# The first projection by input tile: another order of the first loads, of the first matmuls and of VectorE's first work

## What is computed

```python
hn = rms_norm(h, mixer_norm_g[layer])
proj = h @ w_in                                   # 1024 x 2560
q, k, v, g, u = jnp.split(proj, [512, 1024, 1536, 2048], axis=-1)
q = rope(q, positions)                            # t1*cos - t2*sin, t1*sin + t2*cos
k = rope(k, positions) * (Dh ** -0.5)
scores = jnp.einsum('bhncd,bhnmd->bhncm', qc, kc) * decay_mask[:, None]
o_intra = jnp.einsum('bhncm,bhnme->bhnce', scores, vc)
pool_out = multiscale_pool(u, pool_w, pool_scale) # windows of 2, 4, 8, 16 tokens
```

## Times and profile before

| | us |
|---|---|
| median of 3 runs (1122.77 to 1123.47) | 1122.93 |
| profiled execution, device time | 1124.2 |
| its span in the trace | 1122.4 |
| TensorE busy | 1115.6 (99%) |
| VectorE busy | 834.2 (74%) |
| ScalarE busy | 610.5 (54%) |
| GpSimd busy | 44.4 (4%) |
| all DMA queues | 203.53 MB, mean 181 GB/s |

### The profile page before, as it was taken

The page is one execution under the profiler, slowest core; times in us unless marked ns, Lnnn a source line. Parts: engine busy times, 40 slices in busy tenths (PEclk is TensorE's granted clock), DMA queues, the critical chain, the costliest instruction groups (busy, mean ns, idle before and its releaser), DMA issues.

```text
span 1122.4 us, 18843 instructions
## 1 busy us (share of the span) xinstructions
PE 1115.6 (99%) x7338; PEld 995.4 (89%) x7338; DVE 834.2 (74%) x1287; ACT 610.5 (54%) x951; POOL 44.4 (4%) x67
## 2 busy tenths in 40 slices
PE   9999999999999999999999999999999999999998
PEld 9999888888876988888899998888888789888887
DVE  6977877766775878777658867877765887877753
ACT  5645566554541756655543455666544677655631
POOL 4030000000000000000000000000001210000000
PEclk9999999999999999999999999999999999999999
DMA  8545555555483445555544645555654325555552
GB/s 306 189 158 183 175 194 189 195 194 184 154 282 112 151 168 208 188 188 200 210 153 153 223 151 187 188 188 190 220 191 150 136 91 185 186 192 189 181 201 69
DMA packets 35368, 203.53 MB, mean 181 GB/s; under 512 B 4176, under 2 KB 10576, under 8 KB 11984
## 3 DMA queue, kind: packets, MB, share of 16 engines
q1 hardware_dynamic: 35136, 202.32, 51.4%
q10 hardware_dynamic: 144, 0.01, 0.0%
HBM read 200.09 MB, written 2.23 MB: 180 GB/s over the span
## 4 chain that ended last, share of the span: by engine, by line
PE 94%; DVE 3%; DMA 1%; ACT 1%; issue 0%; SPq 0%; DVEq 0%; ACTq 0%
PE banks L421 46%; PE banks L434 24%; PE banks L397 5%; PE banks L403 5%; PE banks L400 5%; PE banks L474 5%; PE banks L457 1%; PE banks L463 1%; PE banks L460 1%; DMA raw_t<-w 1%; DVE lo_t L328 1%; PE banks L1610 0%; DVE lo_t L315 0%; DVE scr L1369 0%; PE banks L1596 0%
## 5 line engine op out<-in xcount | busy, mean ns | idle before, releaser
L328 DVE TENSOR_TENSOR lo_t<-raw_t,hi_t 128x1024 fp32r<-128x1024 f32 x364 | 439.9, 1220 | 11.4 <-ACT hi_t L322 10.3
L322 ACT ACTIVATE hi_t<-raw_t 128x1024 fp32r<-128x1024 f32 x364 | 376.1, 1050 | 106.2 <-PE banks L434 39.1
L421 PE MATMUL banks<-x,hi_t 128*128 128x512 f32 x1536 | 363.4, 391 | 0.0
L421 PEld LDWEIGHTS banks<-x,hi_t 128*128 128x128 f32 x1536 | 284.1, 188 | 57.2 <-issue 0.8
L434 PEld LDWEIGHTS banks<-x,lo_t 128*128 128x128 f32 x1536 | 193.5, 191 | 5.4
L434 PE MATMUL banks<-x,lo_t 128*128 128x256 f32 x1536 | 195.8, 283 | 0.0
L421 PE MATMUL banks<-f,hi_t 128*128 128x512 f32 x704 | 164.1, 390 | 0.0
L421 PEld LDWEIGHTS banks<-f,hi_t 128*128 128x128 f32 x704 | 130.6, 188 | 26.1
L560 DVE TENSOR_TENSOR scr<-banks,scr 128x512 f32<-128x512 f32 x88 | 60.9, 692 | 82.0 <-ACT scr L628 81.3
L434 PEld LDWEIGHTS banks<-f,lo_t 128*128 128x128 f32 x704 | 87.6, 192 | 1.9
L434 PE MATMUL banks<-f,lo_t 128*128 128x256 f32 x704 | 88.2, 283 | 0.0
(11 more groups left out here) (197 smaller groups left out, 1117.6 us busy)
## 6 DMA issues: line engine op xcount, KB each, us to landing
raw_t<-w SPq DMA_DIRECT2D x182, 1024.0 KB, 4.9
scr<-shifts SPq DMA_DIRECT2D x32, 142.0 KB, 4.1
raw_t<-w SPq DMA_DIRECT2D x3, 512.0 KB, 10.2
shifts<-scr SPq DMA_DIRECT2D x8, 144.0 KB, 3.5
h<-xT SPq DMA_DIRECT2D x4, 256.0 KB, 7.7
out<-h SPq DMA_DIRECT2D x8, 128.0 KB, 4.4
cst<-consts SPq DMA_DIRECT2D x1, 816.0 KB, 12.4
raw_t<-w SPq DMA_DIRECT2D x2, 256.0 KB, 5.1
```

The source lines that it names most:

```text
L322: e.activation(hi_t[:, p % RING, :], raw_of(p), ACT.Copy).then_inc(s_hi, 1)
L328: e.tensor_tensor(lo_t[:, p % RING, :], raw_of(p), hi_t[:, p % RING, :].bitcast(F32), ALU.subtract).then_inc(s_lo, 1)
L421: m = e.matmul(halves(banks[:, to[j], :]), hi_t[:, slot, r * P:(r + 1) * P], parts[:, ks[j], :, :], start=ks[j] == 0 and not low_first, st ...
```

## The change

The whole query and key projection is taken by input tile, with eight weight tiles (one piece) for each, into banks 0 to 3. The weights' layout on the host follows (`wide(tiles(...), 8)`). SyncE's list is reordered: x's second, third and fourth transfers go later, the fourth behind chunk 2; the first half piece is issued by ScalarE. The column sums stand before input tile 6, root's spread behind V's first two strips. On VectorE x's low parts 5 to 7 and the low parts of pieces 5 to 8 go between the angle's operations, and the mean as well. ScalarE waits for the columns and the gains' product behind high part 8, where it waits for the angles. The warm-up has 17 matmuls.

```diff
-WARM_START = 21
+WARM_START = 17
...
             e.dma_start(h[:, 0:2, :], xT[:, 0:2, :]).then_inc(s_x[0], 16)
-            e.dma_start(raw_t[:, 0, 0:512], w[0, :, 0:512]).then_inc(s_first[0], 16)
             e.dma_start(raw_t[:, 0, 512:PIECE], w[0, :, 512:PIECE]).then_inc(s_first[1], 16)
-            for n in range(1, EARLY):
...
+            for what in ("w1", "x1", "w2", "w3", "x2"):
...
             load_chunk(e, 2)
+            e.dma_start(h[:, 6:8, :], xT[:, 6:8, :]).then_inc(s_x[3], 16)
...
         def act_start(e):
+            e.dma_start(raw_t[:, 0, 0:512], w[0, :, 0:512]).then_inc(s_first[0], 16)
             e.dma_start(col[:, 0:FIRST_COLS], cols[:, 0:FIRST_COLS]).then_inc(s_col0, 16)
...
                 act_xh(e, 0, k)
-                early_hi(e, k)
-            for p in range(EARLY, RING):
-                split_hi(e, p)
-            e.wait_ge(s_col, 16)
-            e.wait_ge(s_gg, 1)
+                if k < EARLY:
+                    early_hi(e, 2 * k)
+                    early_hi(e, 2 * k + 1)
+                elif k < RING:
+                    split_hi(e, k)
...
         def dve_start(e):
             e.memset(one[:, :], 1.0).then_inc(s_one, 1)
-            for k in range(KD):
+            for k in range(EARLY):
                 dve_xl(e, 0, k)
-                early_lo(e, k)
+                early_lo(e, 2 * k)
+                early_lo(e, 2 * k + 1)
+            dve_xl(e, 0, 4)
             split_lo(e, EARLY)
+            dve_xl(e, 0, 5)
+            lo_to(e, 19)
...
+            dve_xl(e, 0, 6)
+            lo_to(e, 27)
             e.wait_ge(s_col, 16)
...
-            lo_to(e, 19)
+            dve_xl(e, 0, 7)
+            lo_to(e, 35)
+            dve_mean(e, 0)
             for c in (P1, P2, P3, P4):
...
+            lo_to(e, 48)
...
         def pe_first_tiles(e, k):
...
+            for half in range(2):
+                js = range(4 * half, 4 * half + 4)
+                dsts = [banks[:, j // 2, (j % 2) * T:(j % 2 + 1) * T] for j in js]
...
         def pe_retention(e):
             for k in range(KD):
+                if k == 6:
+                    pe_col_sums(e, 0)
                 pe_first_tiles(e, k)
-            for u in range(2, 4):
...
             for k in range(KD):
                 strip(e, G_V + 4 * k, (banks[:, 4, :], banks[:, 5, :]), k, k == 0, k == KD - 1)
+                if k == 0:
+                    pe_spread(e, 0)
...
         def act_retention(e):
             hi_to(e, 35)
+            e.wait_ge(s_col, 16)
+            e.wait_ge(s_gg, 1)
             e.wait_ge(s_angle, 2)
             e.activation(sin, w1, ACT.Sin, scale=colv("sgn", 0))
             e.activation(cos, w0, ACT.Sin).then_inc(s_sines, 1)
-            for u, c in zip(range(4), (51, 59, 67, 75)):
+            for u, c in zip(range(4), (64, 67, 71, 75)):
                 hi_to(e, c)
                 ps = banks[:, u, :]
-                e.wait_ge(s_tiles, upto(16 * max(u, 1) + 15))
+                e.wait_ge(s_tiles, upto(63))
...
         def dve_retention(e):
-            lo_to(e, 48)
-            dve_mean(e, 0)
...
-    parts = [wide(tiles(w_in[:, 0:1024]), 4), flat(strips(w_in[:, 1024:1536])), flat(tiles(w_in[:, 2048:2560])),
+    parts = [wide(tiles(w_in[:, 0:1024]), 8), flat(strips(w_in[:, 1024:1536])), flat(tiles(w_in[:, 2048:2560])),
```

More of the change, by code:

```diff
@@ L727, in act_start @@
             e.activation(st[:, 5, 0:1], one[:, 0:1], ACT.Copy)
+            e.wait_ge(s_col0, 16)
             for k in range(KD):
-                if k == 0:
-                    e.wait_ge(s_col0, 16)
                 if k % 2 == 0:
@@ L814, in pe_first_tiles @@
         def pe_first_tiles(e, k):
-            half, at = k % 2, k // 2 + 1
-            dsts = [banks[:, v, t * T:(t + 1) * T] for v in range(2) for t in range(2)]
-            cols_of = [slice((4 * half + j) * P, (4 * half + j + 1) * P) for j in range(4)]
-            e.wait_ge(s_hi if half else s_hi_half, at)
-            e.wait_ge(s_xh, x_done(0, k))
-            for j in range(4):
-                e.matmul(dsts[j], hi_t[:, k // 2, cols_of[j]], x2[:, k, 0, :], start=k == 0 and j % 2 == 0, stop=False,
-                         skip_group_check=True)
@@ L824, in pe_first_tiles @@
-            e.wait_ge(s_xl, x_done(0, k))
-            for j in range(4):
-                e.matmul(dsts[j], hi_t[:, k // 2, cols_of[j]], x2[:, k, 1, :], start=False, stop=False,
-                         skip_group_check=True)
-            e.wait_ge(s_lo if half else s_lo_half, at)
-            for j in range(4):
-                m = e.matmul(dsts[j], lo_t[:, k // 2, cols_of[j]], x2[:, k, 0, :], start=False, stop=k == KD - 1,
-                             skip_group_check=True)
-            if half:
-                m.then_inc(s_tiles, 1)
+            for half in range(2):
+                js = range(4 * half, 4 * half + 4)
+                dsts = [banks[:, j // 2, (j % 2) * T:(j % 2 + 1) * T] for j in js]
+                cols_of = [slice(j * P, (j + 1) * P) for j in js]
+                early = k < EARLY and half == 0
+                e.wait_ge(s_hi_half if early else s_hi, k + 1)
+                e.wait_ge(s_xh, x_done(0, k))
+                for j, dst, c in zip(js, dsts, cols_of):
+                    e.matmul(dst, hi_t[:, k % RING, c], x2[:, k, 0, :], start=k == 0 and j % 2 == 0, stop=False, skip_group_check=True)
+                e.wait_ge(s_xl, x_done(0, k))
+                for dst, c in zip(dsts, cols_of):
+                    e.matmul(dst, hi_t[:, k % RING, c], x2[:, k, 1, :], start=False, stop=False, skip_group_check=True)
+                e.wait_ge(s_lo_half if early else s_lo, k + 1)
+                for dst, c in zip(dsts, cols_of):
+                    m = e.matmul(dst, lo_t[:, k % RING, c], x2[:, k, 0, :], start=False, stop=k == KD - 1, skip_group_check=True)
@@ L835, in pe_retention @@
+            m.then_inc(s_tiles, 1)
         def pe_retention(e):
             for k in range(KD):
+                if k == 6:
+                    pe_col_sums(e, 0)
                 pe_first_tiles(e, k)
-            for u in range(2, 4):
-                for t in range(2):
-                    for k in range(KD):
-                        c = 16 * u + 8 * t + k
-                        if c == 48:
-                            pe_col_sums(e, 0)
-                        if c == 60:
-                            pe_spread(e, 0)
-                        tile(e, G_QK + c, banks[:, u, t * T:(t + 1) * T], k, x2, k == 0, k == KD - 1)
```

10 lines of the change are left out of this document (6 added, 4 removed).

## The result

The changed kernel took 1127.45 us (median of 5 runs, 1126.72 to 1127.51) beside 1122.93 us for the one before (5 runs, 1122.3 to 1124.24): a ratio of 1.0035 with a 95% interval of 1.0025 to 1.0046, slower by 4.5 us, where 1126.7 was forecast. Timed again later (e8) it took 1125.88 (11 runs) beside 1123.1 (33 runs), a ratio of 1.0023 (1.0014 to 1.0031), slower by 2.8. The profiled execution took 1127.08 with a span of 1125.3, 2.9 over the span before.

A forecast was written before the change was run, and what follows sets the result against it. VectorE's serial chain, not TensorE at 99% busy, was taken as the thin place. Waits of 2.55 at U's first low part, then 0.2, reaching 3.8 in total at PV, took 1122.9 to 1126.7 us; range 1124.3 to 1128.2.

The forecast's parts named there:

- rival A: Chunk 3 lands 1.6 to 2.0 us earlier and VectorE's chain follows one for one: 1124.7 us; chance 0.17.
- its own signs of being wrong: Chunk 3 landing before 23, the table load running before the angles, or VectorE beginning low part 12 before 44.
- Part 1: Shorter warm-up and earlier first values: TensorE starts at 7.7, 0.9 us earlier; columns 0.3 later, hidden; bounds 0 and 1.0.
- the 0.55 of stops at piece 6: TensorE at input tile 6: high part ready at 26.2 against 25.9, and the low part costing 0.25 us.
- Part 2: Order of the input stream: two TensorE stops of 0.3 to 0.7 us stay, at pieces 2 and 4; joint bounds 0 and 1.6.
- Part 3: Landing of the next weights, chunk 3: 25.1 us, bounds 23.1 to 26.1; V begins at 32.2, 2.45 earlier.
- its two terms of 1.5 and 0.4: Lower bound of chunk 3's landing: 1.5 us by which its issue can move up, 0.4 from the first half piece's issue.
- Part 4: VectorE's chain to the sines: angles at 33.4 (now 27.4), table load behind them, low part 9 late by 4.4 us.
- the 0.55 of slack: Before PV in the old kernel: third head's masked scores ready at 72.30, PV matmuls beginning at 72.89.
- B: Faster: input stops were the bound and the angles' chain is not, 1120.5 us; chance 0.06.
- C: TensorE's long stop at U also costs speed, +2.9 us, of which 1.05 lies in VectorE's lag: 1128.5; chance 0.11.
- D: Angles late, but ScalarE's table load out of the chain: -1.3 us, 1125.4, still slower; chance 0.08.

The follow-up runs named there:

- e8: Changed kernel timed again, unaltered, beside the kernel before; 1125.88 us, 1.0023 to the kernel before.
- e2: Changed kernel with a small early sine, so ScalarE loads the sine table ahead of its waits; 1124.24 us, 1.0011 to the kernel before.
- e5: e3 with VectorE's last eight angle operations moved ahead, four before x's low part 6 and four behind low part 6; 1122.21 us, 0.9991 to the kernel before.
- e1: Changed kernel with the first half piece back on SyncE's list, behind x's first transfer; 1125.32 us, 1.0019 to the kernel before.
- e9: Changed kernel with ScalarE issuing the small column load ahead of the first half piece; 1125.58 us, 1.0020 to the kernel before.
- e7: Kernel before with only the warm-up shortened, 17 matmuls for 21; 1122.77 us, 0.9998 to the kernel before.
- e4: Kernel before with only the first half piece issued by ScalarE, ahead of the columns; 1125.73 us, 1.0023 to the kernel before.
- e6: e5 with low parts 12 to 14 earlier among the ropes and 19, 20 in VectorE's waits for GpSimd; 1122.26 us, 0.9989 to the kernel before.
- e3: Changed kernel with the edits of e1 and e2 together; 1123.67 us, 1.0006 to the kernel before.

## Why the prediction was right, and where its terms were not

**Direction and cause: right. Size: near, and in part by luck.** The stretch to PV was forecast 3.8 us longer and is 2.9 longer. The main cause is the one named, VectorE's serial chain with the angles behind the low parts, and ScalarE's table load behind the angles. e2 and e5 show it: each link taken out comes back at PV, 1.35 and 1.47. But 1.05 more comes from the late start, which the prediction had hidden. Without it (e1's start, at full clock behind U) PV would stand 1.9 over before, 75.40 - 0.65 against 72.89, which by the prediction's own scale is 1124.8, rival A's time and not the forecast's. One of its own signs of being wrong also came true: chunk 3 landed before 23. And the waits that it looked for ahead of high and low part 9 are not in TensorE's rows; with V early they are (e1: 0.61 and 0.60).

**Part 1, the start: wrong.** The columns were to be 0.3 us late, with a bound of 1.0, and hidden. They were 3.4 late, and TensorE began at 9.33, not 7.7, though the warm-up did end at 7.64. The step that failed counted the cost of the second queue as 0.3 us, an issue's time. What it left out is what a small transfer pays behind a large one on the same queue: e9 takes that away with one swap. V began at 33.85 instead of 32.2, late by these 1.6 us; the length from the first matmul to V came out as reckoned (24.5), though the 0.55 of stops at piece 6 in it are not there.

**Part 2: within its bounds.** Two stops of 0.3 to 0.7 were forecast. One has a row, 0.46, ahead of a low part at input tile 4; the one at piece 2 is not there, nor is it in e1, where TensorE starts at 7.15.

**Part 3, chunk 3: wrong, without effect.** It landed at 22.50, not 25.1 (bounds 23.1 to 26.1; 25.1 less its two terms of 1.5 and 0.4 is 23.2). The step read the share of 0.99 as "the same bytes take the same time". A share says that the DMA engines are busy, not how much they move: from 9 to 12 us the share was 0.94 before and 1.04 after, and the rate 269 and 424 GB/s. Nor did the full share bear out the bound set beside it, that the landing moves by 0.4 us at most: it moved by 2.8 (25.27 to 22.50).

```profile
9.00:12.00 3.00, 3.00 (x28) 3.00 (x27) 0.83 (x3) 1.39 (x3) 2.02 (x3) 1.00 0.94 269
```
```profile
9.00:12.00 3.00, 2.67 (x22) 2.67 (x23) 3.00 (x4) 3.00 (x7) 2.17 (x4) 1.00 1.04 424
```

The landing also varies without any change to the stream, 25.27 in the profile of before and 24.17 in e7's. SyncE issued the chunk at 14.38, not near 11.5, since the two pieces of chunk 0 were split later.

**Part 4, the chain: its length right, its start right by two errors that cancel, which is luck.** It was to start with chunk 3, low part 6 at 26.2. Chunk 3 was there 3.7 us sooner, but VectorE was not: it had begun at 8.79 and not stood still, its operations beside GpSimd taking up to twice their time (x's low part 0.95, alone 0.48). Low part 6 began at 25.79. From there the working holds: to the last angle operation 6.9 us (7.1), to the high part behind the load 2.0 (2.02), to low part 9 1.15 (1.1). +3.8 instead of +4.4 there is the 0.4 of low part 6's start and the 0.2 of the chain. The spread and piece 9 cost 0.1 us and not 1.9, because V began 1.6 later while the chain was 0.6 earlier; as the prediction has it, all of this is gone at U anyway. The stop at U was 2.12, ahead of PV +3.5 arrived of +3.8, less the 0.55 of slack: 2.9. The 0.3 went into a wait that the prediction had counted as none: before, VectorE stands 0.26 for TensorE at 57.28, and after the change it does not.

**The medians.** At equal mean clock 1.000, on one chip, the changed kernel takes 1125.47 (5 runs) and the one before 1122.93 (20 runs): 2.5 us. With both slow stretches the changed kernel takes 1127.03 (3 runs). In the first measurement all five runs of it had a slow stretch and four had both, hence 4.5; in the second three of eleven had both, hence 2.8. With the 1.2 and 0.65 of the two stretches, 2.5 becomes 4.35 of the 4.5. So the forecast of 3.8 lies between the two levels, and hits the first median closely only because the clock added what the chain did not.

**The rivals.** A (chunk 3 early, and the chain one for one with it): the landing came, the gain did not, since VectorE was held by its own start. With the start repaired (e1) low part 6 does follow the chunk, which lands at 23.57, 1.5 before the forecast's time, and the cost over before is 1.7 at equal mean clock (1124.43 in 4 runs against 1122.70). B (faster): no; even e5, with all links out, gains 0.9 us, not 2.4. C (the stop costs speed too): wrong for the profiled execution, right as a mechanism in at least 21 of 49 runs, four of the first five among them, at a lower price: the stretch from U's first low part to PV takes 28.67 us in e1 and 27.52 in the changed kernel without its last wait, 1.15 more where 2.9 was put, and 0.65 of it is left at PV where 1.85 was put, since the rest goes into that wait. Its remark that the granted clock is 1.00 throughout holds for the rows that it cites, to 27 us; the same trace has 0.50 at 364. D (table load not in the chain): no; e2 is that case, made, and costs 1.3 less, as D was priced.

## What to carry to other kernels

Before work is moved into an engine's stream, ask which other engine waits for what stands behind it, and count that wait with all that it holds up: here the angles moved by 5 us on VectorE, and a table load and three high parts on ScalarE went with them. Use the first function of a new table ahead of the wait for its data. A small transfer on which everything starts goes first on its queue; a stop of TensorE may, in some executions, cost its clock as well as its length. And repair an unrelated delay before judging an order: here the late start hid how early the chunk was there.

## What was not expected of the hardware

- 256 KB ahead of 9 KB on ScalarE's queue delayed the 9 KB by 3.4 us and x's first transfer on SyncE's queue by 2.6 (4.75 to 7.34; in e4 by 1.3, to 6.09); the reverse order delayed both by under 0.4.
- In the changed kernel's profile the DMA engines moved 80 GB/s at a share of 0.64 (4 to 5 us), 129 at 1.02 (3 to 4 us) and 424 at 1.04 (9 to 12 us).
- A stop of 2.2 us was followed, in some executions of the same program and not in others, by 3 us at a granted clock of 0.50; a stop of 0.9 us, and that of 1.7 to 2.1 us ahead of the first real matmul, were not.
- VectorE and GpSimd at once can slow either: a low part of 128 x 1024 takes 1.76 instead of 1.22 at 20.94 in the changed kernel, while in e6 the low part takes 1.22 and GpSimd's two windows beside it 2.26 instead of 1.34.
- The warm-up's passes went from about 0.2 to 0.11 us each at a different time in each execution, from about 4 us (e7) to about 7 us (before, e3, e5), under a granted clock of 1.00 in every row.
